# Projection stage of a hybrid streaming encoder layer: block order, x pieces and the split of a search between VectorE and ScalarE

## The reference

```python
h = jnp.einsum('bld,de->ble', x, w_in)      # x: 2048 prompt and 8 x 16 sample tokens, D = 1024; w_in: 1024 x 5720
z_s, xbc, dtr, q, k, v, z_a, qi, ki, wi = jnp.split(h, cuts, axis=-1)
# SSD branch: causal conv of width 4 over xbc, SiLU, chunked scan with dt = softplus(dtr + dt_bias), gated RMSNorm
# attention branch:
s = einsum('bqhd,bld->bqhl', qi, ki_all) * IDX_DIM ** -0.5
score = einsum('bqh,bql->...', wi * IDX_HEADS ** -0.5, relu(s))        # then -inf where not admissible
top_val, top_idx = lax.top_k(score, k_sel)                             # 256 of up to 2048 keys; 132 for samples
# softmax attention over the chosen keys, times silu(z_a)
y = LN(ALPHA * x + concat([y_ssd, att]) @ w_out)
```

## Time and profile before

| | us |
|---|---|
| median of 3 runs | 3117.33 (3112.48 to 3118.05) |
| span of the profiled execution | 3115.3 |
| TensorE busy | 2719.6 (87%) |
| VectorE busy | 2179.2 (70%) |
| ScalarE busy | 1100.6 (35%) |
| GpSimd busy | 634.8 (20%) |
| projection stage, start to the next stage's first instruction | 452.4 to 1474.7 |

### The profile page before, as it was taken

One profiled execution on the slowest core, in us unless ns is written; L12 is line 12 of the kernel. 1 busy time (PEld: TensorE's weight loads), 2 busy tenths in 40 slices (PEclk: granted clock), 3 DMA queues, 4 the chain that ended last, 5 costly groups with the idle time before them and its releaser, 6 DMA issues. The chain is left out here.

```text
span 3115.3 us, 40926 instructions
## 1 busy us (share of the span) xinstructions
PE 2719.6 (87%) x15348; PEld 2279.6 (73%) x15398; DVE 2179.2 (70%) x3768; ACT 1100.6 (35%) x1970; POOL 634.8 (20%) x694
## 2 busy tenths in 40 slices
PE   6879969999998999996577775899999986599998
PEld 4667539999998888996465653667777765488886
DVE  2326999999999999997688855666666655344333
ACT  2215971112221212212544442555554443232222
POOL 0002002333333333433044532211111000000000
PEclk8869989999999999998699987999999998799999
DMA  5320015222225233346412415211110005522221
GB/s 183 134 83 1 1 58 170 87 89 88 87 87 189 88 102 95 97 142 218 177 41 68 122 45 169 72 41 41 31 31 28 21 20 167 186 93 98 92 81 48
DMA packets 177409, 286.03 MB, mean 92 GB/s; under 512 B 27834, under 2 KB 125890, under 8 KB 173382
## 3 DMA queue, kind: packets, MB, share of 16 engines
q1 hardware_dynamic: 157401, 220.56, 22.4%
q0 software_dynamic: 19824, 62.97, 5.4%
HBM read 177.77 MB, written 105.71 MB: 91 GB/s over the span
## 5 line engine op out<-in xcount | busy, mean ns | idle before, releaser
L705 DVE TENSOR_SCALAR_CACHE_REDUCE project_junk<-all_S,project_cand 128x528 bf16<-128x528 f32 (+7 forms) x256 | 370.0, 1445 | 4.8 <-DVE project_cand L730 4.7
L629 PE MATMUL PS<-project_wh,project_xh 128*128 128x256 f32 x1224 | 348.0, 284 | 8.6 <-POOL project_wl L675 5.7
L629 PE MATMUL PS<-project_xh,project_wh 128*128 128x384 f32 (+1 forms) x880 | 317.0, 360 | 37.9 <-DMA project_xl<-x_parts 37.9
L629 PE MATMUL PS<-project_wl,project_xh 128*128 128x256 f32 x1224 | 347.6, 284 | 0.0
L629 PE MATMUL PS<-project_wh,project_xl 128*128 128x256 f32 x1224 | 347.4, 284 | 0.0
L1601 DVE TENSOR_TENSOR attend_ptl<-PS,attend_pth 128x512 fp32r<-128x512 f32 x272 | 186.3, 690 | 186.9 <-ACT attend_pth L1539 186.0
L629 PE MATMUL PS<-project_xh,project_wl 128*128 128x384 f32 (+1 forms) x880 | 316.3, 359 | 0.0
L629 PE MATMUL PS<-project_xl,project_wh 128*128 128x384 f32 (+1 forms) x880 | 316.0, 359 | 0.0
L705 DVE TENSOR_SCALAR_CACHE_REDUCE project_tie<-all_S,project_cand 128x384 bf16<-128x384 f32 (+6 forms) x224 | 315.7, 1409 | 0.0
L675 POOL TENSOR_TENSOR project_wl<-project_raw,project_wh 128x1024 fp32r<-128x1024 f32 x80 | 201.6, 2541 | 240.4 <-ACT project_wh L642 240.4
L1539 ACT CAST attend_pth<-PS 128x512 fp32r<-128x512 f32 x272 | 157.8, 585 | 242.2 <-PE PS L1486 241.2
(11 more groups left out here) (309 smaller groups left out, 6026.8 us busy)
## 6 DMA issues: line engine op xcount, KB each, us to landing
project_raw<-in_w_in SPq DMA_DIRECT2D x80, 512.0 KB, 4.4
featT<-project_st POOLq DMA_DIRECT2D x66, 192.0 KB, 2.2
featT<-project_st POOLq DMA_DIRECT2D x44, 256.0 KB, 2.3
gate_s<-project_st POOLq DMA_DIRECT2D x68, 128.0 KB, 2.1
gate_a<-project_st POOLq DMA_DIRECT2D x68, 128.0 KB, 2.2
x_conv<-all_S SPq DMA_DIRECT2D x8, 1088.0 KB, 5.3
conv_x<-x_conv SPq DMA_DIRECT2D x8, 1088.0 KB, 6.6
ssd_zs<-gate_s SPq DMA_DIRECT2D x17, 512.0 KB, 4.4
```

The costliest lines, as they stand in the source:

```text
L629: last = nc.tensor.matmul(PS[:, r % 8, 0:w], lhsT, rhs, start=(k == 0 and j == 0), stop=(k == KT - 1 and j == 2))
L705: v.tensor_scalar((junk, tie)[j % 2][:, 0:L], tile_scores(j), th, None, op, ALU.add, accum_out=into[:, j:j + 1]).then_inc(counted, 1)
```

## The change

Five edits, all in `stage_project`:
- In each half the token block for v comes first, then the feature blocks, then the other token blocks. x is loaded in pieces of two tiles, and the matmuls of the v block wait for the piece of their tile.
- `raw` holds two whole blocks. The load of block blk waits for `proj` at `used[blk - 2]`, the end of block blk - 2, where it waited for the low part of block blk - 1. `high` and `low` for the next block are called behind the third group of the current one, where they were called for the block after the next behind the last group. TensorE waits for each half of the weights apart.
- Within an iteration of the search the seven tiles of 1,024 to 1,792 keys are only compared on VectorE, into a ring of four bf16 buffers, and ScalarE sums the ring's buffer. ScalarE does its sums at places fixed by the number of columns projected: iteration i's between columns 1200 + 1728 (i + 0.25) and 1200 + 1728 (i + 0.95).
- The convolution's loads and stores stand at blocks 31 to 36 of SyncE's queue, where they stood at 37 to 39 and behind.
- The bias of dt is added behind the first round of counts, ScalarE's part of softplus stands at the start of block 1, VectorE's behind the masks and ahead of the convolution.

```diff
-        raw = m("raw3", [P, 2, 4, 2 * P])
+        raw = b.map("project", m.end)("raw3", [P, 2, KT, 2 * P])
+        NRING = 4
+        BY_ACT = [j for j in range(NSEL) if 1024 <= keys_of(SEL[j]) <= 1792]
+        NA = len(BY_ACT)
+        ring = m("ring", [P, NRING, 1792], BF16)
...
-        tcols = [C_ZS + 2 * P * i for i in range(4)] + [C_ZA + 2 * P * i for i in range(4)] + [C_V]
+        tcols = [C_ZS + 2 * P * i for i in range(4)] + [C_ZA + 2 * P * i for i in range(4)]
-        cols = fcols + tcols
+        cols = [C_V] + fcols + tcols
...
+        SUM_FIRST, SUM_EVERY = 1200, 1728
+        due = [SUM_FIRST + SUM_EVERY * (i + 0.25 + 0.7 * a / (NA - 1)) for i in range(31) for a in range(NA)]
+        sums_at, cols_done = [], 0
+        for o in outs:
+            cols_done += o[5]
+            sums_at.append([k for k, d in enumerate(due) if cols_done - o[5] < d <= cols_done])
+        CONV_AT = NBLK - 9
...
+                def load_x(hf, k):
+                    t0, (c0, c1) = HALF[hf][0], x_cuts(hf)[k]
+                    if hf:
+                        sp.wait_ge(proj, used[NBLK // 2 - 2] + c1)
...
+                def load_w(blk):
+                    if blk >= 2:
+                        sp.wait_ge(proj, used[blk - 2])
+                    for kh in range(2):
+                        sp.dma_start(raw[:, blk % 2, 4 * kh:4 * kh + 4, :], b.w_rows[:, 4 * kh:4 * kh + 4, cols[blk % len(cols)]:
+                                                          cols[blk % len(cols)] + 2 * P]).then_inc(raw_in[blk % 2][kh], 16)
+                load_w(0)
+                for k in range(3):
+                    load_x(0, k)
+                load_w(1)
+                for k in range(3, 5):
+                    load_x(0, k)
+                for blk in range(2, NBLK):
+                    if blk == NBLK // 2 + 2:
+                        for k in range(4):
+                            load_x(1, k)
+                    if blk == CONV_AT:
                         sp.wait_ge(sel, SEL_STEPS)
...
+                    if CONV_AT + 2 <= blk < CONV_AT + 2 + XF // 2:
+                        store_conv(2 * (blk - CONV_AT - 2))
+                        store_conv(2 * (blk - CONV_AT - 2) + 1)
+                    load_w(blk)
...
-                    pe.wait_ge(w_hi, 2 * blk + 2)
-                    pe.wait_ge(w_lo, 2 * blk + 2)
+                        if n == 0:
+                            k = (i - HALF[hf][0]) // 2
+                            pe.wait_ge(x_in[k], 32 * (hf + 1 if k < 4 else 1))
                         for k in range(KT):
+                            if r == first and k % 4 == 0:
+                                pe.wait_ge(w_hi, 2 * blk + k // 4 + 1)
+                                pe.wait_ge(w_lo, 2 * blk + k // 4 + 1)
...
+                        for k in sums_at[r]:
+                            j, s = BY_ACT[k % NA], k % NA % NRING
+                            act.wait_ge(compared, k + 1)
+                            nc.scalar.activation(ring[:, s, 0:keys_of(SEL[j])], ring[:, s, 0:keys_of(SEL[j])], ACT.Copy,
+                                                 accum_out=count[:, j:j + 1]).then_inc(summed, 1)
                         r += 1
-                    high(blk + 2)
+                        if blk and r == used[blk - 1] + 3:
+                            high(blk + 1)
...
+                def shared_counts(i):
+                    for j in turns:
+                        L, th = keys_of(SEL[j]), candf[:, j:j + 1]
+                        if j in BY_ACT:
+                            a = BY_ACT.index(j)
+                            if a >= NRING:
+                                dve.wait_ge(summed, i * NA + a - NRING + 1)
+                            v.tensor_scalar(ring[:, a % NRING, 0:L], tile_scores(j), th, None, ALU.is_ge
+                                            ).then_inc(compared, 1)
+                        else:
+                            n = mine.index(j)
+                            dve.wait_ge(counted, NSEL + i * len(mine) + n)
+                            v.tensor_scalar(junk[:, 0:L], tile_scores(j), th, None, ALU.is_ge, ALU.add,
+                                            accum_out=count[:, j:j + 1]).then_inc(counted, 1)
+                    dve.wait_ge(counted, NSEL + i * len(mine) + len(mine))
+                    dve.wait_ge(summed, i * NA + NA)
...
-                    counts(NSEL + i * NSEL, candf, ALU.is_ge, count)
+                    shared_counts(i)
```

More of the change, by code:

```diff
@@ L496, in stage_project @@
         xp = [m("xh3", [P, KT, HW], F32R), m("xl3", [P, KT, HW], F32R)]
-        raw = m("raw3", [P, 2, 4, 2 * P])
-        wp = [m("wh3", [P, 2, KT, 2 * P], F32R), m("wl3", [P, 2, KT, 2 * P], F32R)]
+        raw = b.map("project", m.end)("raw3", [P, 2, KT, 2 * P])
+        wp = [m("wl3", [P, 2, KT, 2 * P], F32R)]
+        wp = [m("wh3", [P, 2, KT, 2 * P], F32R)] + wp
         st = m("st3", [P, 4, 512])
         dtb, aneg = m("dtb", [P, H]), m("aneg", [P, H])
-        soft = b.map("softplus", m.end)
-        sp_e, sp_u, sp_d, sp_l = (soft(n, [P, TILES + 1, H]) for n in ("sp_e", "sp_u", "sp_d", "sp_l"))
+        sp_e, sp_l = m("sp_e", [P, TILES + 1, H]), b.a
+        sp_u = b.last3[:, :, :].rearrange("p f c -> p (f c)")[:, 0:(TILES + 1) * H].rearrange(
+            "p (t h) -> p t h", h=H)
         up = S[:, (SALL + 1) // 2:]
@@ L514, in stage_project @@
         count, want, above, room = (m(n, [P, NSEL]) for n in ("count", "want", "above", "room"))
-        raw_in = [sem("raw_in0"), sem("raw_in1")]
+        raw_in = [[sem(f"raw_in{s}{kh}") for kh in range(2)] for s in range(2)]
         w_hi, w_lo = sem("w_hi"), sem("w_lo")
-        x_in = [sem(f"x_in{i}") for i in range(3)]
+        x_in = [sem(f"x_in{i}") for i in range(5)]
         proj, proj_out = sem("proj"), sem("proj_out")
@@ L536, in stage_project @@
             for n in range(len(cols)):
-                if n < NF:
-                    for f in (2 * n, 2 * n + 1):
+                if 1 <= n <= NF:
+                    for f in (2 * n - 2, 2 * n - 1):
                         for c0, w in even_pieces((t1 - t0) * P):
@@ L551, in place, with x_cuts @@
                 return b.featT[i, :, HALF[hf][0] * P + c0:HALF[hf][0] * P + c0 + w]
-            if n == NF + 8:
+            if n == 0:
                 return b.v_s if i == ST else b.v_p[i * P:(i + 1) * P, :]
-            g = (b.gate_s, b.gate_a)[(n - NF) // 4]
-            return g[i * P:(i + 1) * P, ((n - NF) % 4) * 2 * P:((n - NF) % 4 + 1) * 2 * P]
+            z = n - NF - 1
+            g = (b.gate_s, b.gate_a)[z // 4]
+            return g[i * P:(i + 1) * P, (z % 4) * 2 * P:(z % 4 + 1) * 2 * P]
+        def x_cuts(hf):
+            t0, t1 = HALF[hf]
+            return [(c, min(c + 2, t1 - t0)) for c in range(0, t1 - t0, 2)]
+        SUM_FIRST, SUM_EVERY = 1200, 1728
[4 more added lines that the diff above has]
+            sums_at.append([k for k, d in enumerate(due) if cols_done - o[5] < d <= cols_done])
+        assert sum(map(len, sums_at)) == 31 * NA
+        CONV_AT = NBLK - 9
         with nc.Block() as block:
@@ L582, in _ @@
                     sp.dma_start(dst[:, :], b.ins[src].partition_broadcast(P)).then_inc(dt_in, 16)
-                for blk in range(NBLK):
-                    if blk == NBLK - 3:
+                def load_w(blk):
[4 more added lines that the diff above has]
+                                                          cols[blk % len(cols)] + 2 * P]).then_inc(raw_in[blk % 2][kh], 16)
@@ L603, in _ @@
-                for f in range(4, XF):
-                    store_conv(f)
+                    if CONV_AT + 2 <= blk < CONV_AT + 2 + XF // 2:
+                        store_conv(2 * (blk - CONV_AT - 2))
+                        store_conv(2 * (blk - CONV_AT - 2) + 1)
+                    load_w(blk)
                 for i in range(2):
@@ L612, in _ @@
                     hf, n = blk // len(cols), blk % len(cols)
-                    pe.wait_ge(w_hi, 2 * blk + 2)
-                    pe.wait_ge(w_lo, 2 * blk + 2)
+                    first = r
                     while r < used[blk]:
@@ L685, in _ @@
                         r += 1
-                    low(blk + 2)
+                        if blk and r == used[blk - 1] + 3:
+                            low(blk + 1)
                 for i in range(4):
@@ L706, in counts @@
                                         accum_out=into[:, j:j + 1]).then_inc(counted, 1)
+                mine = [j for j in range(NSEL) if j not in BY_ACT]
+                turns = []
+                for j in range(max(len(mine), NA)):
+                    turns += BY_ACT[j:j + 1] + mine[j:j + 1]
+                def shared_counts(i):
[14 more added lines that the diff above has]
+                    dve.wait_ge(summed, i * NA + NA)
                 v.memset(want[:, 0:1], float(TOPK_S))
@@ L743, in _ @@
                 dve.wait_ge(sel, 1)
-                counts(32 * NSEL, candf, ALU.is_gt, above)
-                dve.wait_ge(counted, 33 * NSEL)
```

(3 more changed lines are left out.)

103 lines of the change are left out of this document (43 added, 60 removed).

## The result

The changed kernel takes 3120.7 us (median of 16 runs, 3116.5 to 3125.1), the kernel before 3114.2 beside it (16 runs, 3108.5 to 3118.1): ratio 1.0021, interval 1.0013 to 1.0028. It is slower, by 6.5 us. No change was forecast, at 3117; the time lies in the range. The forecast started from 3117.3, the median of three runs of the kernel before, which is 3.1 above that of the sixteen.

The account below looks back on a forecast made before the run. The projection stage was taken to run on TensorE, with only 67.6 us beyond its matmuls to win. Losses of 12.8 + 4.4 + 12.9 + 6 + 24.5 + 6.9 = 67.5 left 3117 us, no change; range 3105 to 3135.

Parts of the forecast that it names:

- the stall at block 31: SyncE holds block 31's weights until the last mask is done; TensorE loses 24.5 us, low clock included.
- the refill: Between halves, half 2's x queues behind w(21), which waits for all of block 19: 12.9 us lost.
- start: Smaller first loads: first matmul at 465.2 instead of 468.0 us, half 1 over at 977.5 instead of 988.0.
- tail: From TensorE's last matmul to the stage's end, with softplus moved to block 1: 6.9 us instead of 17.6.
- the sum of the stage: Projection stage's losses add to 67.5 us against 67.6 before, so it ends at 1474.5 instead of 1474.7.
- the late casts: Groups of 512 columns, blocks 22 to 24: weights cast behind due sums come late, 6 us in all, bounds 0 and 10.
- the masks and the restart behind them: Last mask 147.3 us behind the last sum; block 31's first weight half split 16.2 us behind the mask.
- Nothing behind the stage changes: Stages after the projection keep their times, so the total is 3117 us, no change.
- Rival B: VectorE, held up by GpSimd in the split search, can't keep TensorE's pace: 14 us slower, 3131; chance 0.30.
- C: ScalarE's sums nearer 1.05 us, one weight window misses the masks, casts come in time: 9 us faster, 3108; chance 0.20.
- D: Block 31's weights aren't held because the masks are done by 1221: 24.5 us faster, 3093; chance 0.05.
- The signs named for the forecast: First matmul at 465, idle on x after block 19, small idles at blocks 22 to 24, some 24 us at block 31.

Follow-up runs that it names:

- e4: Changed kernel with half 2's x ahead of block 21's weights and the convolution's loads at block 33 instead of 31: 3081.8 us, projection stage 992.3.
- e6: Changed kernel with half 2's x ahead of block 21's weights, convolution at block 33, casts behind the second group in four-group blocks: 3065.6 us, projection stage 982.2.
- e1: Changed kernel with half 2's x loads one block earlier in SyncE's queue, ahead of block 21's weights: 3107.4 us.
- e8: Changed kernel with softplus put back behind the convolution, its ScalarE part at the head of the last block: 3118.4 us.

## Why the prediction was wrong, and where it was right

The mechanism was the forecast's: the stall at block 31 and the refill ate what start and tail gave. What failed is the sum of the stage, which came to 1022.1 us, as long as before, and measured 1032.6. Its biggest miss is the term for the late casts, "I take 6 us in all, bounds 0 and 10": it measured 10.1 us (the stage of e4 against that of e6), and 9.4 in the changed kernel. Of the other 7.1 us, 2.1 are in the start, 2.1 in the refill, 2.2 in the masks and the restart behind them, 0.7 behind block 31's start. Two things had no price there: the low clock behind an idle time (start, late casts), which the prediction charged only at block 31, and the uneven halves of a split (restart).

That the time is only 3.7 us from the forecast is luck. The stage's error of 10.5 met two others of opposite sign: a starting number 3.1 too high, and a scan stage some 5 us shorter, which no term had.

Measured from each stage's start (452.4 in the prediction, 453.9 after):

| event | predicted | measured | step's error |
|---|---|---|---|
| first matmul | 12.8 | 13.1 | +0.3 |
| end of half 1 | 525.1 | 527.2 | +1.8 |
| half 2's feature blocks begin | 561.0 | 565.2 | +2.1 |
| search's last sum in | 643.6 | 651.2 | +3.4 |
| last mask | 790.9 | 799.5 | +1.0 |
| block 31 starts | 807.1 | 816.9 | +1.2 |
| TensorE ends | 1015.2 | 1025.6 | +0.6 |
| stage ends | 1022.1 | 1032.6 | +0.1 |

- **Start, +2.1 in all.** The low clock behind the wait for the second wave of x was left out: the granted clock is 0.67 from 488.8 to 494.0, so the 5.2 us do the work of 3.5. These are 1.7 of the 2.1. The first line below shows it; the second is from the refill and the third from behind the late casts:

```profile
488.80:494.00 5.20, 5.20 (x31) 5.20 (x32) 0.00 (x0) 1.25 (x4) 1.16 (x3) 0.67 0.64 193
...
992.80:1006.00 13.20, 13.18 (x92) 13.20 (x93) 4.29 (x9) 3.97 (x8) 1.62 (x3) 0.82 1.10 353
...
1091.80:1106.00 14.20, 14.18 (x53) 11.53 (x54) 11.05 (x16) 6.98 (x10) 4.46 (x3) 0.83 0.10 38
```

- **Refill, +2.1.** The rate held (353 GB/s from 992.8 to 1006; 364 was used). The DMA engines move 26 GB/s until 982.5, 1.4 us behind the end of half 1, and the full rate ends near 1010.7, so the stream takes 28.3 us, and 28.6 was forecast. But the matmul that waits for the last piece starts at 1013.05. So 1.4 us ahead of the stream and 2.3 behind it stand against 1.5 in the sum. The low clock of 0.82 in this stretch adds nothing, since TensorE waits for the last piece all the same. That half 2 waits behind w(21) was right, and e1 shows that it is the whole wait.
- **Late casts, +3.4.** The count gave idle times of 2.5, 0.6 and 1.4 us, with room for more; they are 1.97, 0.43 and 4.53, 6.9 in all. Behind the last the granted clock is 0.83 for 14.2 us, which costs 2.4 more and had no price here. The prediction counted sums and casts in ScalarE's order, as if every compare were ready. It bounded the collisions by 4.8 us per block, took 3.0, and spent them as an average over an iteration; here they fell on the head of two iterations, where ScalarE has no compare ready to sum.
- **Masks and restart, +1.0 and +1.2.** The same code took 148.2 instead of 147.3, and TensorE started 17.4 behind the mask instead of 16.2. Cast and split began 11.5 and 12.7 behind the mask, no later than before (11.7 and 12.8). But the first half of the split took 4.63 of the 6.96 us of both. The sum had taken half of 6.65, while before, too, the first half took 4.3 of them: the second starts at 1379.65.
- **Tail.** Predicted 6.9, found 7.0, but the text put it down to softplus alone. By e8 softplus's new place gives nothing here, and the convolution's gives all.
- **Nothing behind the stage changes.** Wrong by some 5 us, in the other direction; with the stage's 10.5 us alone on top of 3114.2 the time would have been near 3125. It comes with the granted clock of the scan stage, as shown above.

Rival B (VectorE can't keep pace, 3131) named the right collision, but half 1 shows no idle time on weights. Only groups of 512 columns, with one group between cast and need, let it through; that half 1's slack covers it is argued, not tested. Its price was 14 us; at most 4 of it came (10.1 against 6). C failed on the mask and the casts, though one of its conditions held: the sums cost 1.06 to 1.70 us, not 1.15 to 1.80. D is refuted by the stall. The signs named for the forecast were there, and half 1 ended at 981, ahead of the bound of 985; but ScalarE's waits on compares, named for B, were there too.

What stays open is why the clock falls behind the same idle time of the scan stage in nine profiles and not in the three of the changed kernel and e8. TensorE's work ahead of it, in the same stage, is the same in all twelve to within 2 us. No run was made inside that stage, so neither the program ahead of it nor chance is shown as the cause.

## What to carry to other kernels

Load order decides more here than the work saved: two numbers in SyncE's queue (x one block earlier, the convolution two blocks later) are worth 39 us, while the 97 us by which the search got shorter are worth less than nothing until they are set right. When work moves ahead, look for what waits for it in the same queue: a wait on the masks that cost 5.7 us at block 37 cost 23.7 at block 31. When two operations that hinder each other are released by neighbours in one engine's program, they can meet again and again, and a busy share says nothing of it: here the cast and the iteration's last sum should stand apart. And price the low clock behind each idle time of some microseconds, not only behind the longest.

## What the runs showed of the hardware

- Two VectorE operations on 15 elements a row took 2.34 and 2.33 us, where 0.17 is usual, since each met a half of GpSimd's split (2.35 us each); one compare of 1,024 keys took 5.70 instead of 0.75 beside both halves (4.77 us). So a small operation lost about as much as the other's instruction takes.
- ScalarE sums bf16 rows in place at 1.06 us for 1,024 and 1.70 for 1,792 elements, and 0.19 more to read the sum.
- Behind an idle time of 2.1 us, after the same 1,138 matmuls, TensorE's granted clock was 1.00 in three profiles and 0.52 to 0.70 in nine. An unchanged stage of 1,538 matmuls took 350.9 to 356.8 us with it, so a change of under 6 us in a total can't be put down to an edit without looking at the stages that it left alone.
